# Opening each stage's first four outputs from un-normed tiles, and the second mixer's head norms with tokens on the partitions

## The reference, cut to what matters

```python
def first_block(x, ...):                    # i = 0: rwkv mixer, i = 1: gated deltanet mixer
        x = _layer_norm(DEEPNORM_ALPHA * x + (1 + ga1) * y, ln_g[i, 0], ln_b[i, 0])
        u = x * (1 + sc2) + sh2
        gate, up = jnp.split(u @ ffn_w_in[i], 2, axis=-1)
        y = (jax.nn.silu(gate) * up) @ ffn_w_out[i]
        x = _layer_norm(DEEPNORM_ALPHA * x + (1 + ga2) * y, ln_g[i, 1], ln_b[i, 1])
def _gated_deltanet_mixer(...):             # its head norms
    q = _l2norm(qkv[..., :hd].reshape(B, T, H, d)) * d ** -0.5
    k = _l2norm(qkv[..., hd:2 * hd].reshape(B, T, H, d))
    o = _rms_norm(o, norm_g, 1e-6) * jax.nn.silu(z.astype(F32))
def second_block(x, meta, ...):
    for l in range(DEPTH):
        h = layer_norm(ALPHA * h + 0.5 * swiglu(h, ...), ln1_g[l], ln1_b[l])
        # proj = h @ w_in[l]; three mixers; mix = their outputs @ w_out[l]
        h = layer_norm(ALPHA * h + mix, ln2_g[l], ln2_b[l])
        h = layer_norm(ALPHA * h + 0.5 * swiglu(h, ...), ln3_g[l], ln3_b[l])
```

## Time and profile before

| what | us |
|---|---|
| three runs | 2302.4, 2307.1, 2310.05 (median 2307.1) |
| the profiled execution, its own time | 2305.64 |
| its span | 2303.7 |
| PE busy, share of the span | 2112.9 (92%) |
| DVE busy | 1224.2 (53%) |
| ACT busy | 869.2 (38%) |
| POOL busy | 708.9 (31%) |
| mean granted PE clock | 0.958 of full speed |

### The profile page before, as it was taken

One profiled execution on the slowest core, in us unless ns is written; L12 is line 12 of the kernel. 1 busy time (PEld: TensorE's weight loads), 2 busy tenths in 40 slices (PEclk: granted clock), 3 DMA queues, 4 the chain that ended last, 5 costly groups with the idle time before them and its releaser, 6 DMA issues.

```text
span 2303.7 us, 40612 instructions
## 1 busy us (share of the span) xinstructions
PE 2112.9 (92%) x17634; PEld 1904.4 (83%) x17634; DVE 1224.2 (53%) x2205; ACT 869.2 (38%) x1258; POOL 708.9 (31%) x316
## 2 busy tenths in 40 slices
PE   4989988999988989999999898899999998989997
PEld 3867866889887867898999895699989997857897
DVE  6166445763673347653642666555264418457652
ACT  0442111454443223543433444343343334434543
POOL 0350001314573003126314560131561175304124
PEclk9998998999999899999999998899999998979999
DMA  8564442455343003554444340245435453304552
GB/s 330 220 274 148 149 163 75 150 184 188 141 147 128 2 1 128 188 196 166 160 170 180 131 147 19 92 169 180 167 145 179 169 177 108 119 19 147 184 191 83
DMA packets 49681, 340.43 MB, mean 148 GB/s; under 512 B 6368, under 2 KB 8416, under 8 KB 8672
## 3 DMA queue, kind: packets, MB, share of 16 engines
q1 hardware_dynamic: 49504, 337.84, 40.6%
HBM read 336.77 MB, written 1.05 MB: 147 GB/s over the span
## 4 chain that ended last, share of the span: by engine, by line
PE 81%; DVE 12%; ACT 3%; issue 2%; POOL 1%; DMA 1%; SPq 0%; ACTq 0%; POOLq 0%; DVEq 0%
PE bank L531 80%; POOL ring_low L2485 1%; DMA ada_ring<-ada 1%; DVE arena L1873 1%; DVE arena L1901 1%; PE bank L537 1%; DVE arena L1858 1%; ACT high L1446 1%; DVE small L1868 1%; DVE arena_parts L1896 1%; DVE arena L1888 0%; DVE ZZ L2082 0%; DVE small L2340 0%; DVE small L2451 0%; DVE acc L1963 0%
## 5 line engine op out<-in xcount | busy, mean ns | idle before, releaser
L531 PE MATMUL bank<-arena_parts,high 128*128 128x272 f32 (+2 forms) x4512 | 1026.4, 315 | 61.2 <-ACT arena_parts L1471 38.0
L531 PEld LDWEIGHTS bank<-arena_parts,high 128*128 128x128 f32 x4512 | 749.8, 191 | 111.6 <-issue 48.8
L531 PE MATMUL bank<-arena_parts,ring_low 128*128 128x272 f32 (+2 forms) x2736 | 782.1, 288 | 0.0
L1446 ACT ACTIVATE high<-ring 128x2048 fp32r<-128x2048 f32 x237 | 453.1, 1914 | 679.5 <-PE bank L531 593.5
L2485 POOL TENSOR_TENSOR ring_low<-ring,high 128x2048 fp32r<-128x2048 f32 x105 | 485.3, 4626 | 697.3 <-ACT high L1446 697.3
L531 PEld LDWEIGHTS bank<-arena_parts,ring_low 128*128 128x128 f32 (+1 forms) x2736 | 523.7, 191 | 1.0
L1909 DVE TENSOR_TENSOR ring_low<-ring,high 128x2048 fp32r<-128x2048 f32 x132 | 303.6, 2300 | 181.1 <-ACT high L1446 181.1
L531 PE MATMUL bank<-hidden_high,high 128*128 128x256 f32 (+1 forms) x1056 | 303.2, 287 | 0.0
L531 PE MATMUL bank<-hidden_low,high 128*128 128x256 f32 (+1 forms) x1056 | 301.1, 285 | 0.0
L531 PE MATMUL bank<-hidden_high,ring_low 128*128 128x256 f32 (+1 forms) x1056 | 300.1, 284 | 0.0
L2485 POOL TENSOR_TENSOR hidden_low<-arena,hidden_high 128x256 fp32r<-128x256 f32 (+1 forms) x132 | 111.8, 849 | 575.4 <-DVE hidden_high L1925 575.4
(11 more groups left out here) (327 smaller groups left out, 2262.7 us busy)
## 6 DMA issues: line engine op xcount, KB each, us to landing
ring<-stream SPq DMA_DIRECT2D x269, 1024.0 KB, 4.8
ada_ring<-ada SPq DMA_DIRECT2D x48, 1024.0 KB, 6.2
...
```

Source lines behind the costliest of these rows:

```text
L531: ins = nc.tensor.matmul(o, l, r, start=start, stop=stop_, skip_group_check=True)
L1446: act(high[:, q % HIGHS], ring[:, s % RING], ACT.Copy).then_inc(a.sig(high_ready), 1)
```

## The change

**Opened raw.** For n = 0, 1, 2, 4, 5, 6, 7, 8 (`OPENED_RAW`; not norm 3) `raw_four` takes the place of `first_four`. Its inputs are un-normed tiles, (x - shift) * gain: ACT makes the rounded one (`raw_tile`) behind each square, DVE the rest (`raw_rest`, one instruction with both inputs in SBUF). Behind a mixer (norms 0, 2, 5, 8) three of the eight rests stand among the last residuals and five inside `norm`; behind an FFN seven and one. Four extra columns carry gain and bias. PE makes the mean's last sum and the squares' sum inside `raw_four`. It waits for the normed tiles only at f = 2 (at `gdn_ba` and `dtf` in the other stages).

**Scaled afterwards.** DVE scales the four results in the banks (`scale_opened`: a reduce of 4 columns, one or two scalar_tensor_tensor, one tensor_tensor) ahead of SiLU or `convolve`.

**Operands.** The squares go to SBUF (`staged`) in place of banks 1 and 2. `less_shift` of tiles 4 to 7 and `center` read SBUF copies in place of banks 3 and 4.

**Order.** The normed tiles' ACT and DVE steps wait for `opened` (PE done with the raw tile whose place they take). The eight L1901 (`residual_base`) move behind f = 1, or behind the third convolution, in stage 3 to the start of `ffn`. ACT makes high(q0+2) at the start of `norm_out` and high(q0+3) in quarters between tiles 2 to 5. POOL has no wait for `input_low` and does q0+2 and q0+3 back to back; DVE starts at q0+4.

**Head norms.** `token_sums` sums with the squares as the stationary operand and one moving column, so tokens come out on the partitions; scale factors are a 128x16 tile; `spread_scale` spreads with 128-column matmuls; the multiplication by gain and gate goes ahead of the scale, in four parts.

```diff
+OPENED_RAW = (0, 1, 2, 4, 5, 6, 7, 8)
+RAW_WIDTH = META + SEQ + 4
+RAW_HIGH_AT = {n: 7 * DT * TALL if n == 0 else 4 * DT * TALL + 6 * TALL for n in OPENED_RAW}
+RAW_LOW_SLOT = {n: 2 if n in (5, 8) else 1 for n in OPENED_RAW}
...
-    return STAGES[n] == "ffn" and HIGHS <= q - STAGE_AT[n] < HIGHS + FT
+    return STAGES[n] == "ffn" and HIGHS < q - STAGE_AT[n] < HIGHS + FT
...
-    def norm(T):
-        t0 = xview(T)
+    def mean_sum(T):
+        residual(8)
+        mm(bank[4][:, 0:T], cm("mean"), tl(XAS, 7, T, xview(T)), False, True, hold=True).then_inc(told(4, "vector"), 1)
...
+    def square_sum(T):
         eng.wait_ge(*freed(5))
...
         mm(bank[5][:, 0:T], cm("mean"), square_sums(T), True, False)
-        residual(8)
-        mm(bank[4][:, 0:T], cm("mean"), tl(XAS, 7, T, t0), False, True, hold=True).then_inc(told(4, "vector"), 1)
         eng.wait_ge(squared, pe.nth(squared, 8))
-        mm(bank[5][:, 0:T], cm("mean"), tl(9, 7, T), False, True, hold=True).then_inc(told(5, "vector"), 1)
...
+    def raw_four(n, tiles, T, signals):
...
+        for k in range(DT):
+            eng.wait_ge(raw_high_ready, pe.nth(raw_high_ready))
...
+            blocks = [split_block((*tile, k)) for tile in tiles]
+            both, low = raw_both(n, k, T), raw_low(n, k, T)
+            if k == DT - 1:
+                for b, (w_high, w_low) in enumerate(blocks):
+                    m = mm(bank[b][:, 0:T], w_high, low, False, False, hold=b == 3)
+                m.then_inc(opened, 1)
+            for b, (w_high, w_low) in enumerate(blocks):
+                if k == 0 and b == 2:
+                    mean_sum(T)
+                mm(bank[b][:, 0:T + 4], w_high, both, k == 0, False)
+                m = mm(bank[b][:, 0:T + 4], w_low, both, False, k == DT - 1, hold=k == DT - 1)
+                if k == DT - 1:
+                    m.then_inc(signals[b], 1)
+            if k == 0:
+                square_sum(T)
+            if k < DT - 1:
+                for b, (w_high, w_low) in enumerate(blocks):
+                    m = mm(bank[b][:, 0:T], w_high, low, False, False, hold=b == 3)
+                m.then_inc(opened, 1)
...
+    def normal_tile():
+        eng.wait_ge(input_high_ready, pe.nth(input_high_ready))
+        eng.wait_ge(input_low, pe.nth(input_low))
...
+    def token_sums(src_slot, b):
...
+        for h in range(DT):
+            for c in range(2):
+                m = mm(bank[b][:, 2 * h + c:2 * h + c + 1], tl(src_slot, h)[:, P * c:P * c + P], one[:, :],
+                       True, True, hold=h == 7 and c)
...
+    def spread_scale(i, banks):
...
+                m = mm(bank[b][:, o:o + P], head_scale[:, i, h, c:c + 1].to_broadcast([P, P]), ident,
+                       True, True, hold=h % 2 and c)
...
-    row_sums(8, 4, "vector", "hsel8", 8)
-    row_sums(3, 5, "vector", "hsel8", 8)
+    token_sums(8, 4)
+    token_sums(3, 5)
     eng.wait_ge(v2p, pe.nth(v2p))
-    spread(small[:, 2, 0:SEQ], "sel12", P, B4)
-    spread(small[:, 1, 0:SEQ], "sel12", P, B4)
...
-            to = bank[1 + j % 2][:, 0:T] if j else square_sums(T)
+            to = staged[:, j % 2, 0:T] if j else square_sums(T)
...
+            if raw:
+                raw_tile(n, j, T)
...
-        act(tl(9, 7, T), tl(9, 7, T), ACT.Square).then_inc(a.sig(squared), 1)
+        act(staged[:, 2, 0:T], tl(9, 7, T), ACT.Square).then_inc(a.sig(squared), 1)
+        if raw:
+            raw_tile(n, 7, T)
...
-        act(small[:, 0, 0:T], small[:, 0, 0:T], ACT.Square).then_inc(a.sig(shift_squared), 1)
+        act(small[:, 2, 0:T], small[:, 0, 0:T], ACT.Square).then_inc(a.sig(shift_squared), 1)
...
+    def raw_tile(n, j, T):
+        act(raw_high(n, j, T), tl(9, j, T), ACT.Copy, scale=lnc[:, n, 0, j:j + 1]).then_inc(a.sig(raw_high_ready), 1)
...
+    def quarter_high(q, i):
...
+        act(high[:, q % HIGHS, part], ring[:, HL[q] % RING, part], ACT.Copy).then_inc(a.sig(high_ready if i == 3 else astep), 1)
...
+    def norm_out(n, T):
+        raw = n in OPENED_RAW
+        weights_high(STAGE_AT[n] + 2)
...
+            if raw:
+                eng.wait_ge(opened, done + min(j + 2, DT - 1))
...
+            if raw and 2 <= j < 6:
+                quarter_high(STAGE_AT[n] + HIGHS, j - 2)
...
+    def raw_rest(n, js, T):
...
+            nv.scalar_tensor_tensor(out=raw_low(n, j, T), in0=tl(9, j, T), scalar=lnc[:, n, 0, j:j + 1],
+                                    in1=raw_high(n, j, T).bitcast(F32), op0=ALU.mult,
+                                    op1=ALU.subtract).then_inc(v.sig(raw_low_ready), 1)
...
         def less_shift(j):
-            nv.tensor_tensor(tl(9, j, T), tl(XAS, j, T, t0), bank[3][:, 0:T], ALU.subtract).then_inc(v.sig(centered), 1)
+            shift = bank[3] if j < 4 else small[:, 1]
+            nv.tensor_tensor(tl(9, j, T), tl(XAS, j, T, t0), shift[:, 0:T], ALU.subtract).then_inc(v.sig(centered), 1)
...
-            nv.tensor_tensor(squares, squares, bank[1 + j % 2][:, 0:T], ALU.add).then_inc(v.sig(square_added), 1)
+            nv.tensor_tensor(squares, squares, staged[:, j % 2, 0:T], ALU.add).then_inc(v.sig(square_added), 1)
...
-        def center(q):
-            x = arena[:, XAS, 2 * q:2 * q + 2, t0:t0 + T]
-            nv.tensor_tensor(x, x, over_tiles(bank[4][:, 0:T], 2, T), ALU.subtract).then_inc(v.sig(vstep), 1)
...
+        nv.tensor_tensor(small[:, 0, 0:T], small[:, 1, 0:T], bank[4][:, 0:T], ALU.subtract).then_inc(v.sig(shift_ready), 1)
...
+        def center(q):
+            x = arena[:, 9, 2 * q:2 * q + 2, 0:T]
+            nv.tensor_tensor(x, x, over_tiles(small[:, 0, 0:T], 2, T), ALU.add).then_inc(v.sig(vstep), 1)
...
+        if raw:
+            done = v.nth(opened, DT) - DT
...
+                if raw:
+                    eng.wait_ge(opened, done + j + 1)
+                nv.tensor_scalar(tl(US, j, T, xview(T)), tl(9, j, T), lnc[:, n, 0, j:j + 1], lnc[:, n, 1, j:j + 1],
                                  ALU.mult, ALU.add).then_inc(v.sig(vstep), 1)
...
+    def residual_base(n, T):
         for j in range(DT):
-            nv.tensor_scalar(tl(XAS, j, T, t0), tl(9, j, T), lnc[:, n, 2, j:j + 1], lnc[:, n, 3, j:j + 1],
+            nv.tensor_scalar(tl(XAS, j, T, xview(T)), tl(9, j, T), lnc[:, n, 2, j:j + 1], lnc[:, n, 3, j:j + 1],
                                   ALU.mult, ALU.add).then_inc(v.sig(base_ready if j == DT - 1 else vstep), 1)
...
+    def scale_opened(b, T, signal, to_bias):
+        both = bank[b][:, T:T + 4].rearrange("p (a e) -> p a e", e=2)
+        nv.tensor_reduce(opening_cols[:, b], both, AX_X, ALU.add).then_inc(v.sig(vstep), 1)
+        eng.wait_ge(*v.last)
+        product = bank[b][:, 0:T]
+        for i in range(1 if to_bias else 2):
+            nv.scalar_tensor_tensor(out=product, in0=small[:, i, 0:T], scalar=opening_cols[:, b, i:i + 1], in1=product,
+                                    op0=ALU.mult, op1=ALU.add).then_inc(v.sig(vstep), 1)
+            eng.wait_ge(*v.last)
+        nv.tensor_tensor(product, product, small[:, 2, 0:T], ALU.mult).then_inc(v.sig(signal), 1)
...
+            if f < 2 and raw:
+                eng.wait_ge(gate_full, full_gate + f + 1)
+                scale_opened(2 * f, T, gate_scaled, True)
+                eng.wait_ge(up_full, v.nth(up_full))
+                scale_opened(2 * f + 1, T, vstep, True)
+                eng.wait_ge(silu_ready, v.nth(silu_ready))
+                eng.wait_ge(*v.last)
+                for to, signal in ((tl(6, f, T), vstep), (hidden_high(f, T), hidden_ready)):
+                    nv.scalar_tensor_tensor(out=to, in0=up, scalar=opening_cols[:, 2 * f + 1, 1:2],
+                                            in1=silu_t[:, f % 2, 0:T], op0=ALU.add, op1=ALU.mult).then_inc(v.sig(signal), 1)
+                gate_halves(f, T)
+                weights_low(q0 + HIGHS + 1 + f)
+                if f == 1:
+                    residual_base(n, T)
+                continue
...
         eng.wait_ge(full_for_vector[b], v.nth(full_for_vector[b]))
+        if n < 4:
+            scale_opened(b, T, vstep, False)
+            eng.wait_ge(*v.last)
...
+        if n == 2:
+            residual_base(1, SEQ)
+            eng.wait_ge(*v.last)
+            nv.memset(arena[:, 9, 0], 0.0).then_inc(v.sig(vstep), 1)
+            nv.memset(arena[:, 9, 4], 0.0).then_inc(v.sig(v2a), 1)
...
+    for i in range(2):
+        eng.wait_ge(full_for_vector[4 + i], v.nth(full_for_vector[4 + i]))
+        nv.tensor_scalar(head_scale[:, i], bank[4 + i][:, 0:16].rearrange("p (h c) -> p h c", c=2), 1.0, 1e-6,
...
         q0 = STAGE_AT[n]
         weights_low(q0)
         weights_low(q0 + 1)
-        eng.wait_ge(input_low, g.nth(input_low, DT))
         weights_low(q0 + 2)
+        weights_low(q0 + 3)
```

More of the change, by code:

```diff
@@ L701, in ffn @@
                             for k in range(DT):
+                                if f == 2 and b == g and raw:
+                                    normal_tile()
                                 w_high, w_low = split_block((name, layer, n, k))
@@ L708, in ffn @@
```

(42 more changed lines are left out.)

264 lines of the change are left out of this document (169 added, 95 removed).

## The result

The changed kernel takes 2377.2 us (median of 4 runs, 2372.7 to 2379.7) against 2306.9: 1.031 times as long (95% interval 1.028 to 1.034). I had forecast 2356, in a range of 2272 to 2388, and slower. The profiled execution has a span of 2373.9, 70.2 more than before.

A forecast was written before the change was run, and what follows sets the result against it. PE's rate was taken to bound the kernel (busy 92%). Terms 8.1 + 0.7 + 3.4 + 15.6 + 28.2 + 2.0 - 7.8 = +50.2 on 2305.6 gave 2355.8, predicted as 2356 us, range 2272 to 2388.

The forecast's parts named there:

- R: Time at which DVE starts the last residual of a norm; later events are counted from it in us.
- rival 1: Normed tiles: POOL's slabs cause no holds on DVE, tiles at R+15.4; sum -33.7, 2272; chance 0.26.
- Q: Experiments' theory: DVE's added work and waits for opened tiles make the normed tiles late, whatever POOL does.
- H: Experiments' theory: DVE instructions with all operands in SBUF are held by POOL's slabs.
- 2.6 to 4.1: Norms behind an FFN: holds by POOL's q0 and q0+1 around the last residuals, 2.6 to 4.1 us each.
- +2.0: Norm 3, not raw: POOL's q0+2 holds the tiles by 4.3, about half hidden; +2.0 us (0 to 4.3).
- +1.4: FFN norms 0, 2, 8: DVE's scalings, moved base and q0+4 delay f=5's hidden tile; +1.4 us (0 to 3.5).
- +2.7: Each of stages 0, 2, 8: +1.3 for f=2 ending later and +1.4 for f=5's wait.
- rival 3: Ahead of f=2's late tiles PE idles about 6 us, then runs at half clock; up to +26, 2382; no separate chance.
- 15.6: Norm 1, gdn: late tiles count in full, with holds, scalings and base included; +15.6 us.
- +14.1: Norms 4 and 7, mixer: 8.9 + 1.3 + 2.6 + 1.3, +14.1 us each.
- 2 (one hold): Normed tiles: q0+2 holds DVE, q0+3 comes after the last tile; +13.1, 2319; chance 0.12.

The follow-up runs named there:

- Runs 4: Kernel before, nothing raw: ACT makes high(q0+2) ahead of the normed tiles and POOL subtracts it without waiting for input_low; 2330.5 us.
- run 11: Against a 2288.9 us kernel with five FFN norms raw and DVE subtracting FFN q0+2: POOL's wait before q0+3 dropped in FFN stages; 2306.9 us.
- Run 2: Changed kernel, but ACT writes the squares of tiles 1 to 6 into PSUM banks 2 and 5; 2366.8 us.
- run 1: Changed kernel, but POOL again waits for the eight input_low before q0+2, and so q0+3; 2353.3 us.
- Run 6: Changed kernel with POOL's wait; behind an FFN, squares and shifts use PSUM banks and all raw rests follow the last residual; 2334.3 us.
- run 3: Kernel before with only the head norms' part of the change; 2300.8 us, ratio 0.9959.

## Why the prediction was right, and what it sized wrong

**Right: the mechanism, and its size at the tiles.** DVE is held twice, 3.7 and 4.2 beyond the pairs' own 0.75, the last tile comes 23.9 behind R (forecast 24.3), the opening ends at R+12.7. Runs 4 and 11 show the hold by itself, run 11 in a kernel that differs in POOL's order alone. Run 2 shows the other half, that an operand in PSUM frees the instruction. With the two slabs out of the way (run 1) the tile is at R+16.0 (my rival 1 said 15.4), so Q explains 1.8 of the 9.7, H the rest. The total is closer than its terms: in the profiled execution stages 0, 3, 5 and 6 took 26 over the forecast and gdn 9 under it.

**Mis-sized: the holds ahead of the last residual.** I put 2.6 to 4.1 for q0 and q0+1 into norms 1, 4, 6 and 7 and 0 for norm 3. POOL and DVE of the changed kernel at the end of stage 0:
```profile
603.03 9.33 POOL L2703 TENSOR_TENSOR ring_low<-ring,high 128x2048 fp32r<-128x2048 f32 x2 [5.47 <-ACT high L1565]
```
```profile
603.13 9.51 DVE L1976 TENSOR_TENSOR acc<-acc,XX 128x256 f32<-128x256 f32 x2
612.56 1.66 DVE L1958 SCALAR_TENSOR_TENSOR arena_parts<-arena,lnc,arena_parts 128x256 fp32r<-128x256 f32 x4
614.15 0.47 DVE L1992 SCALAR_TENSOR_TENSOR arena<-bank,mod,arena 128x256 f32<-128x256 f32 x1
```
Both holds are whole (9.51 for two adds), stand in DVE's queue ahead of the last residual, and PE waits for it: 5.3 at norm 1 and 4.5 each at 4, 6 and 7, where I had let them delay only the first center. That is 5.3 + 3 x 4.5 = 18.8 against 12.6. It is most of what stages 0, 3, 5 and 6 took over the forecast. Run 6, which clears this stretch, gave 19.0 back.

**Mis-sized: norm 3.** +2.0 in the forecast; stage 3 took +11.0. 4.5 is norm 4's residual. The rest is norm 3's own: its reciprocal came at R+5.5 in place of R+3.2 (a slab reached past R and held a shift for 2.8), and the whole hold of POOL's q0+2 showed, where I took half as hidden.

**Swapped: clock and queue.** The forecast put +1.4 for a wait at f=5 and nothing for the clock. No wait came: from f=2's last tile on (433.19) PE had no gap over 0.6 for over 30 us. But f=2 began at half clock, and its last 20 matmuls took 5.45 (433.19 to 438.64) where the row of before gives 3.5: +1.9. f=2 ended at R+29.1, not R+27.5. The two errors nearly cancel (stage 2: +2.8 against +2.7), which is luck. This much of rival 3 was true, though the sign I gave for it, a gap like the 4.15, was not the one: the matmul at 424.42 takes 0.47 and its like at 427.01 takes 0.72, with gaps of only 1.20 and 1.64 before them and the gap of 4.60 still to come. What the late half clock cost in all is not separated: PE's busy time shows only the balance, +14.8, with the 2.0 saved at each opening and the extra matmuls in it.

**Over-sized: lateness that counts in full.** For gdn and the mixers I took DVE's lateness one for one as PE's. The lateness itself was near: the first decay row starts at R+48.1 where it was at R+35.6, so 12.5 later, and 12.2 and 12.9 later in the mixers, against my 13 to 16. But PE's idle time in gdn rose by 6.1 only (26.7 with the heads alone, run 3, to 32.8), and in the mixers by 11.0 and 9.1; PE had other work for the rest. In gdn that is 6.1 for 15.6. That the mixers came at +14.8 and +12.3 against +14.1 is in part luck: PE's busy time was 3.8 and 3.2 higher there, of which the clock's scatter is not separated, and 2.6 of each 14.1 stood for holds whose wait fell into the stage before.

**The rivals.** Rival 1 (no holds) and 2 (one hold) are out by the timeline: both slabs fell among the tiles. POOL's slab reached 5.15 at most where it takes 4.61, so it lost about half a us, as if it waited for the DVE instruction under way, and DVE then waited for all of POOL's. The cost is lopsided since one instruction is ten times the other. The Trainium skill ("SBUF — State Buffer", section "Who interferes with whom") says that whichever of the two engines issues first has the shared pair for its whole instruction, and the other blocks. With that the trace agrees.
